# Nine norm statistics in two rounded passes, with the queries' products moved forward and the shared key squares added by GpSimd

## What is computed

```python
def rms_norm(x, gain):
    xf = x.astype(jnp.float32)
    y = xf * lax.rsqrt(jnp.mean(xf * xf, axis=-1, keepdims=True) + RMS_EPS)
    return (y * gain.astype(jnp.float32)).astype(x.dtype)

q_d = rms_norm(heads(d_q, DSA_HEADS), dsa_q_norm)
k_d = rms_norm(heads(d_k, DSA_HEADS), dsa_k_norm)
q_m = heads(rms_norm(m_cq, mla_q_latent_norm) @ mla_w_uq, MLA_HEADS)
k_rope = jnp.broadcast_to(m_kr[:, :, None, :], (B, S, MLA_HEADS, MLA_ROPE_DIM))
q_m = rms_norm(q_m, mla_q_norm)
k_m = rms_norm(jnp.concatenate([k_nope, k_rope], axis=-1), mla_k_norm)
```

## Time and profile before

| | |
|---|---|
| median of three runs | 1244.68 us (1244.66 to 1244.74) |
| the profiled execution: its own time | 1245.98 us |
| the profiled execution: span, first to last instruction | 1244.2 us |
| PE busy in the span | 1232.3 us (99%) |
| DVE, ACT, POOL busy | 757.9 us (61%), 534.4 us (43%), 232.9 us (19%) |
| granted clock of PE | 0.998 of full speed |
| chain that ended last | PE 92%, DVE 3%, ACT 3%, issue 1%, DMA 1% |

### The profile page before, as it was taken

The page is one execution under the profiler, slowest core; times in us unless marked ns, Lnnn a source line. Parts: engine busy times, 40 slices in busy tenths (PEclk is TensorE's granted clock), DMA queues, the critical chain, the costliest instruction groups (busy, mean ns, idle before and its releaser), DMA issues.

```text
span 1244.2 us, 17723 instructions
## 1 busy us (share of the span) xinstructions
PE 1232.3 (99%) x5952; PEld 973.4 (78%) x5952; DVE 757.9 (61%) x1229; ACT 534.4 (43%) x869; POOL 232.9 (19%) x156
## 2 busy tenths in 40 slices
PE   8999999999999999999999999999999999999998
PEld 7767876788888888888886678757888888888887
DVE  6788978644544554544758899685445445445444
ACT  5675448644223224224437653595442242232331
POOL 1035430020120110210520544201202102002002
PEclk9999999999999999999999999999999999999999
DMA  6312220024223223223222222101223223222323
GB/s 232 102 51 68 73 81 2 23 97 132 87 99 100 96 91 101 101 84 101 101 87 84 68 68 85 52 2 51 85 101 102 85 102 101 89 97 100 100 96 108
DMA packets 30721, 108.37 MB, mean 87 GB/s; under 512 B 3536, under 2 KB 3536, under 8 KB 30672
## 3 DMA queue, kind: packets, MB, share of 16 engines
q1 hardware_dynamic: 29520, 103.82, 24.9%
q0 software_dynamic: 432, 2.86, 0.6%
q10 hardware_dynamic: 720, 1.07, 0.3%
HBM read 105.64 MB, written 2.10 MB: 87 GB/s over the span
## 4 chain that ended last, share of the span: by engine, by line
PE 92%; DVE 3%; ACT 3%; issue 1%; DMA 1%; ACTq 0%; DVEq 0%
PE bank L957 19%; PE bank L955 19%; PE bank L956 19%; PE bank L564 6%; PE bank L565 6%; PE bank L566 6%; PE bank L587 2%; PE bank L585 2%; PE bank L586 2%; PE bank L837 1%; PE bank L849 1%; PE bank L600 1%; PE bank L864 1%; PE bank L711 1%; PE bank L815 1%
## 5 line engine op out<-in xcount | busy, mean ns | idle before, releaser
L1010 ACT ACTIVATE wh<-raw 128x1024 fp32r<-128x1024 f32 x191 | 201.7, 1056 | 371.4 <-PE bank L957 246.5
L1341 DVE TENSOR_TENSOR wl<-raw,wh 128x1024 fp32r<-128x1024 f32 x161 | 248.0, 1540 | 76.9 <-ACT wh L1010 76.9
L955 PE MATMUL bank<-hh,wl 128*128 128x512 f32 x512 | 200.0, 391 | 0.0
L955 PE MATMUL bank<-xmh,wl 128*128 128x512 f32 x512 | 199.3, 389 | 0.0
L957 PE MATMUL bank<-hl,wh 128*128 128x512 f32 x512 | 199.2, 389 | 0.0
L957 PE MATMUL bank<-xml,wh 128*128 128x512 f32 x512 | 199.2, 389 | 0.0
L956 PE MATMUL bank<-xmh,wh 128*128 128x512 f32 x512 | 199.2, 389 | 0.0
L956 PE MATMUL bank<-hh,wh 128*128 128x512 f32 x512 | 199.2, 389 | 0.0
L529 POOL TENSOR_TENSOR x<-x,rsb 128x512 f32<-128x512 f32 x62 | 82.0, 1322 | 587.3 <-DVE rsb L1772 587.3
L1761 DVE TENSOR_TENSOR sqb<-tf 128x512 f32<-128x512 f32 x64 | 44.3, 692 | 180.9 <-ACT hh L1305 180.9
L564 PE MATMUL bank<-xgh,wl 128*128 128x512 f32 x368 | 151.6, 412 | 2.8 <-DVE xgl L1354 2.8
(11 more groups left out here) (231 smaller groups left out, 1677.2 us busy)
## 6 DMA issues: line engine op xcount, KB each, us to landing
raw<-in_stream SPq DMA_DIRECT2D x191, 512.0 KB, 3.3
out_y<-x SPq DMA_DIRECT2D x8, 256.0 KB, 3.8
x<-in_x ACTq DMA_DIRECT2D x4, 256.0 KB, 7.1
x<-in_x SPq DMA_DIRECT2D x4, 256.0 KB, 7.1
con<-in_consts POOLq DMA_DIRECT2D x1, 976.5 KB, 5.1
par<-in_params POOLq DMA_DIRECT2D x1, 916.0 KB, 5.2
par<-in_params POOLq DMA_DIRECT2D x1, 896.0 KB, 6.7
raw<-in_stream SPq DMA_DIRECT2D x2, 256.0 KB, 3.9
```

The source lines that it names most:

```text
L955: pe.matmul(B.t[s][:], wl[:, s, n_block(k)], src_h[:, k], start=(k == 0), stop=False)
L1010: act.activation(wh[:, s], raw[:, s], ACT.Copy).then_inc(hi_ready.sem, 1)
L1341: vec.tensor_tensor(wl[:, s], raw[:, s], wh[:, s], ALU.subtract).then_inc(lo_ready.sem, 1)
```

## The change

1. `FIRST_PART` goes from 7 to 3 and `N_PARTS` from 5 to 9: the statistics `mqst0`, `dqst1`, `mqst1` and `dkst0` take the rounded form too. ACT gets one rounding and DVE one `square_low` for each, and PE two float32r matmuls in place of one float32 matmul.
2. The key squares: `turn_rows`, its three memsets and the float32 matmul of line 666 go. ACT squares the shared rotary rows twice into a new buffer `krq` (rows 0 to 31 and 64 to 95, POOL zeroes the rest), POOL adds `krq` to the squares `sqb` of `mk0` and `mk1` (behind its low part of u = 13 and 14), and only then does ACT round them.
3. DVE's order: a new function `queries_of(u)` runs between `evacuations(u)` and `select_steps`. It holds `mla_queries`, `mla_turn` and the `square_low` of u = 9 to 12. `dsa_queries`, `dsa_keys` and all of u = 13 and 14 but `mla_queries(3)` stay in `tasks(u)`, behind the selection.

The diff without the lines that only follow from these:

```diff
-FIRST_PART, N_PARTS = 7, 5
-ACT_LINKS = 2 + N_PARTS
+FIRST_PART, N_PARTS = 3, 9
+ACT_LINKS = 2 + N_PARTS - 2
...
+        krq, _ = place("krq", [P, T], at=gvt0)
-        turn_rows, _ = place("turn_rows", [P, P])
...
# POOL
-                pool.memset(cqn[QK:P, 1], 0.0).then_inc(padded.sem, 1)
+                pool.memset(cqn[64:P, 1], 0.0).then_inc(padded.sem, 1)
                 pool.wait_ge(*padded.at(l, 1))
                 alone(pool)
+                pool.memset(krq[:], 0.0).then_inc(padded.sem, 1)
+                pool.wait_ge(*padded.at(l, 2))
+                alone(pool)
...
+                    if u in (13, 14):
+                        i = norm_index(f"mkst{u - 13}")
+                        pool.wait_ge(*krsq_ready.at(l, 1))
+                        pool.wait_ge(*ksq_ready.at(l, u - 13))
+                        pool.tensor_tensor(sqb[:, i % 2], sqb[:, i % 2], krq[:], ALU.add).then_inc(ksq_summed.sem, 1)
                     if u in (14, 15):
                         key_end(u - 14)
...
# PE
                 def mla_k_stat(pr):
-                    pe.wait_ge(*krsq_ready.at(l, 0))
                     pe.wait_ge(*B.vacant(l, name))
-                    pe.matmul(B[name][:], turn_rows[:], cqn[:, 1], start=True, stop=False)
                     pe.wait_ge(*nsl_ready.at(l, i - FIRST_PART))
-                    pe.matmul(B[name][:], blk_r[:], sqh[:, i % 2], start=False, stop=False)
+                    pe.matmul(B[name][:], blk_r[:], sqh[:, i % 2], start=True, stop=False)
...
-                stat(l, "dqst1", blk, sq_of("dqst1"))
+                stat_parts(l, "dqst1", blk_r[:]).then_inc(*B.on_fill("dqst1"))
-                stat(l, "dkst0", blk, sq_of("dkst0"))
+                stat_parts(l, "dkst0", blk_r[:]).then_inc(*B.on_fill("dkst0"))
...
# ACT
+                def key_square(pr):
+                    i = norm_index(f"mkst{pr}")
+                    act.wait_ge(*B.filled(l, f"mk{pr}"))
+                    act.activation(sqb[:, i % 2], B[f"mk{pr}"][:], ACT.Square).then_inc(ksq_ready.sem, 1)
+                    act.wait_ge(*ksq_summed.at(l, pr))
+                    act.activation(sqh[:, i % 2], sqb[:, i % 2], ACT.Copy).then_inc(nsq_ready.sem, 1)
...
                         act.wait_ge(*kr_ready.at(l, 0))
-                        act.activation(cqn[64:QK, 1], kT[64:QK, 0], ACT.Square).then_inc(krsq_ready.sem, 1)
+                        act.wait_ge(*padded.at(l, 2))
+                        act.activation(krq[0:ROPE], kT[64:QK, 0], ACT.Square).then_inc(krsq_ready.sem, 1)
+                        act.activation(krq[64:QK], kT[64:QK, 0], ACT.Square).then_inc(krsq_ready.sem, 1)
...
# DVE
-            vec.memset(turn_rows[0:64], 0.0).then_inc(rows_ready.sem, 1)
-            vec.memset(turn_rows[64:QK], 1.0).then_inc(rows_ready.sem, 1)
-            vec.memset(turn_rows[QK:P], 0.0).then_inc(rows_ready.sem, 1)
...
+                def queries_of(u):
+                    if 10 <= u <= 13:
+                        mla_queries(u - 10)
+                    if 9 <= u <= 12:
+                        mla_turn(u - 9)
+                        square_low(f"mqst{u - 9}", slice(0, QK))
+                    if u == 9:
+                        square_low("dqst1")
+                    if u in (10, 11):
+                        square_low(f"dkst{u - 10}")
...
                     evacuations(u)
                     if 6 <= u < POOL_LOW[0]:
                         low_part(u % 2, hi_ready.at(l, u + AHEAD))
+                    queries_of(u)
                     select_steps(done, per_slot.get(u, 0))
                     done += per_slot.get(u, 0)
                     tasks(u)
```

More of the change, by code:

```diff
@@ L237, in build_trunk @@
         ke, ke0 = place("ke", [P, 2, TB, 256])
-        gvt, _ = place("gvt", [P, TB, GLA_H * GLA_DV])
+        gvt, gvt0 = place("gvt", [P, TB, GLA_H * GLA_DV])
+        krq, _ = place("krq", [P, T], at=gvt0)
         e1, _ = place("e1", [P, 2, T])
@@ L346, in build_trunk @@
         rows_ready = S("rows_ready", 0)
-        padded = S("padded", 2)
+        padded = S("padded", 3)
+        ksq_ready = S("ksq_ready", 2)
+        ksq_summed = S("ksq_summed", 2)
         cq_summed = S("cq_summed")
@@ L360, in build_trunk @@
         nrs_used = S("nrs_used", N_NORM, start=2)
-        krsq_ready = S("krsq_ready")
+        krsq_ready = S("krsq_ready", 2)
         krg_ready = S("krg_ready")
@@ L646, in mla_q_stat @@
                 def mla_q_stat(h):
-                    if norm_index(f"mqst{h}") < FIRST_PART:
-                        stat(l, f"mqst{h}", ones[0:QK, 0:QK], sq_of(f"mqst{h}")[0:QK], QK)
-                        return
                     pe.wait_ge(*blk_ready.at(0, 0))
@@ L736, in _ @@
                 pe.wait_ge(*B.vacant(l, "cqst"))
-                pe.wait_ge(*rows_ready.at(0, 3))
+                pe.wait_ge(*rows_ready.at(0, 0))
                 pe.matmul(B["cqst"][:], ones[:], sqb[:, 0], start=True, stop=True).then_inc(*B.on_fill("cqst"))
@@ L1074, in square_high @@
                     act.activation(sqh[rows, i % 2], sqb[rows, i % 2], ACT.Copy).then_inc(nsq_ready.sem, 1)
+                def key_square(pr):
[4 more added lines that the diff above has]
+                    act.activation(sqh[:, i % 2], sqb[:, i % 2], ACT.Copy).then_inc(nsq_ready.sem, 1)
                 def query_square(h):
-                    sq = square if norm_index(f"mqst{h}") < FIRST_PART else square_high
-                    sq(f"mqst{h}", B[f"mq{h}"][0:QK, :], slice(0, QK), wait=B.filled(l, f"mq{h}"))
+                    square_high(f"mqst{h}", B[f"mq{h}"][0:QK, :], slice(0, QK), wait=B.filled(l, f"mq{h}"))
                     if h == 0:
@@ L1170, in tasks @@
                         factor("dqst0", DH)
-                        square("dqst1", dqr[:, 1], wait=B.freed(l, "dq1"))
+                        square_high("dqst1", dqr[:, 1], wait=B.freed(l, "dq1"))
                     if u == 10:
@@ L1175, in tasks @@
                         factor("dqst1", DH)
-                        square("dkst0", dkn[:, 0], wait=B.freed(l, "dk0"))
+                        square_high("dkst0", dkn[:, 0], wait=B.freed(l, "dk0"))
                     if u == 11:
@@ L1187, in tasks @@
                         factor("mqst3", QK, QK)
-                        square_high("mkst0", B["mk0"][:], wait=B.filled(l, "mk0"))
+                        key_square(0)
                     if u == 14:
-                        square_high("mkst1", B["mk1"][:], wait=B.filled(l, "mk1"))
+                        key_square(1)
                     if u in (14, 15):
@@ L1566, in tasks @@
                     if u == 9:
-                        mla_turn(0)
                         dsa_queries(0)
                     if u == 10:
-                        mla_queries(0)
-                        mla_turn(1)
                         dsa_queries(1)
                     if u == 11:
-                        mla_queries(1)
-                        mla_turn(2)
-                        square_low("mqst2", slice(0, QK))
                         dsa_keys(0)
-                        square_low("dkst1")
                     if u == 12:
-                        mla_queries(2)
-                        mla_turn(3)
-                        square_low("mqst3", slice(0, QK))
                         dsa_keys(1)
                     if u == 13:
-                        mla_queries(3)
                         vec.wait_ge(*B.filled(l, "krot"))
```

1 line of the change is left out of this document (removed).

## The result

The changed kernel takes 1262.43 us in the median (1261.94 to 1263.55), against 1244.68 before: a ratio of 1.0144 with a 95% interval of 1.0128 to 1.016. It is slower, as forecast, but by 17.8 us where 7.6 were forecast, and outside the range of 1240 to 1257.5. The profiled execution took 1261.94 us with a span of 1260.1, so the two profiled spans differ by 15.9 us.

A forecast was written before the change was run, and what follows sets the result against it. PE was taken as the bound. A layer loses 2.2 us by `mkst1`, 1.4 at the banks and 0.2 at unit 5: 3.8, or 7.6 in all, giving 1253.6 profiled and 1252.3 for the runs; range 1240 to 1257.5.

The forecast's parts named there:

- PE's saving if it never waits: Four statistics from 0.86 to 0.46 us and two keys' statistics without their float32 matmul: 3.3 us a layer, 6.7 in all.
- The kind of loss: PE idle for DVE's `sql`, 2 us and more a layer, `mla_v` waiting for DVE, DVE instructions held beside POOL.
- The rival of the full gain: PE served in time, POOL's work falling beside the selection: 4.8 to 6.2 us faster, 1238.5 to 1240 us; chance 0.2.
- The 0.2 us at unit 5: ACT's second square of the shared rows delays unit 5's block: PE waits 0.2 us a layer, bounds 0.1 and 0.4.
- `mkst1` gives back: At the second key's statistic the low part is in time and PE wins 0.87 us, leaving 2.2 lost a layer.
- `mla_k(1)` starts 0.6 later [...] 3.0 us lost: At `mkst0` the low part ends at 120.3, PE comes at 117.8, `mla_k(1)` starts at 120.9 instead of 117.85.
- the early branch at `mkst0`: DVE's low part of `mkst0` runs ahead of POOL's next one and ends at 120.3: 3.0 us lost a layer.
- the branch that it priced at 5 us a layer: POOL's next low part, from 119.2, gets ahead of `mkst0`'s low part, which then ends at 122.4: 5 us.
- One layer is worked out and doubled: Layer 1 repeats layer 0 614.4 us later, so 3.8 us lost a layer becomes 7.6 in all.
- I estimate 1.4 us for both: `mv0` and `mv1` wait for the keys' banks, as DVE and ACT's factor come later: 1.4 us a layer, bounds 0 and 3.
- The walk of the two queues: DVE's and POOL's queues followed instruction by instruction with the rows' durations, giving ready times where PE waits; 3.8 us lost a layer.
- the later branches: `dsa_queries(1)` behind POOL's low part, `mkst0`'s low behind the next: 5 to 6 us a layer, 1255 to 1257.5 us; chance 0.18.

The follow-up runs named there:

- e7: Changed kernel plus 7, 7 and 12 idle matmuls in PE's waits at `mqst3`, `mkst0` and `mla_v(1)`: 1264.47 us.
- e14: Changed kernel, DVE making POOL's low parts of units 9 to 12, `mkst0`'s low part and ACT's factor earlier, selection thinned there: 1247.75 us.
- e12: Changed kernel, POOL's low parts of units 9 to 15 halved, `mkst0`'s low part before unit 13's selection, ACT's factor before the wait for POOL's addition: 1245.84 us.
- e2: Kernel before plus the key squares' part alone, with five norms in parts and the old DVE order: 1253.01 us.
- e13: Complete changed kernel, `mkst0`'s low part before unit 13's selection and ACT's factor before the wait for POOL's second addition: 1256.09 us.
- e5: Kernel before plus the key squares alone, ACT making `mkst0`'s factor before waiting for POOL's second addition: 1246.11 us.
- e11: Changed kernel with one edit, ACT making `mkst0`'s factor before waiting for POOL's second addition: 1259.53 us median, profiled execution 1253.46.
- e3: Kernel before plus nine rounded statistics alone, old DVE order, new `square_low` behind the selection, `turn_rows` kept: 1256.37 us.
- e9: Changed kernel without key squares, `mkst0`'s rotation and low part before unit 13's selection, selection steps moved from units 9, 11, 12, 13 to 21, 22: 1254.33 us.
- e10: Complete changed kernel, ACT's factor first, `mkst0`'s low part before unit 13's selection, selection steps moved from units 9, 11, 12, 13 to 21, 22: 1264.01 us.
- e16: Changed kernel, DVE making low parts of units 9 to 12, selection thinned, `mkst0` low part, ACT factor and `mla_keys(1)` earlier, one POOL scaling later: 1244.17 us.

## Why the prediction was wrong in size

**What held.** PE's saving if it never waits, 3.3 us a layer: the nearest run to it (1241.04 us) keeps 2.24 at `mla_v(1)`, with small waits at each step. The kind of loss: PE waits at L672 and L682 for DVE, and DVE's held instructions end 0.55 us after POOL's, in all 21 cases of the two layers' blocks in which one took over 1 us. The rival of the full gain named the right condition, that POOL's work and DVE's miss each other; it took half of POOL's low parts away and three orders to meet it. The 0.2 us at unit 5 held too: in all thirteen kernels with the key squares' part the lateness grows by 0.26 to 0.28 us at that unit of layer 1, and in none of the others.

**By terms**, against the forecast of 3.8 us lost a layer (us; the lateness of the table, in its order):

| term of the sum | forecast | layer 0 | layer 1 |
|---|---|---|---|
| up to `mla_k(1)`: the wait for `mkst0` | 3.05 | 4.32 | 6.04 |
| `mkst1` gives back | -0.87 | -0.87 | -0.87 |
| waits for the banks of `mla_v(0)`, `mla_v(1)` | 1.4 | 3.7 | 0.6 |
| half clock behind them or behind `mkst0` | none | 1.7 | 1.7 |
| unit 5 and small rest | 0.2 | 0.4 | 0.0 |
| sum | 3.8 | 9.23 | 7.47 |

The row for the banks is what is left of the growth of lateness from `mla_k(1)` to `mla_v(1)` when the gain of `mkst1` and, in layer 1, the half clock are taken off. So of the 9.1 us that the two layers together were off, 4.3 were missed at `mkst0`, 3.4 in the clock and 1.5 at the banks.

**The first step that failed: "`mla_k(1)` starts 0.6 later [...] 3.0 us lost".** It took the early branch at `mkst0`, in which DVE's low part is not held, for both layers. Its own times speak for the other: a low part that ends at 120.3 starts at 119.6, and POOL's next low part was to start at 119.2, which is ahead of it. That is the branch that it priced at 5 us a layer, and layer 1 took it: POOL started 0.67 us ahead, DVE took 2.71 us, PE waited 4.7 us, and 6.04 were lost. DVE's line and POOL's in the changed kernel, layer 1:

```profile
743.36 2.71 DVE L1440 TENSOR_TENSOR sql<-sqb,sqh 128x512 fp32r<-128x512 f32 x1
```

```profile
742.69 2.84 POOL L505 TENSOR_TENSOR wl<-raw,wh 128x1024 fp32r<-128x1024 f32 x1 [4.58 <-ACT wh L1014]
```

That layer 0 took the early branch was luck: the stretch of half clock at 112.0, which the prediction did not have, held POOL's low part back to 120.65, behind the 120.00 of DVE's. Layer 1 had the same wait of 1.5 us at `mqst3` and no stretch behind it. "One layer is worked out and doubled" could not see this.

**The second: the clock was no term.** Three stretches of 1.2 GHz at 1.7 us each are 5.1 us of PE's time, and two of them reached the end. The one at 112.0 did not: PE still waited 1.36 us at `mkst0` behind it, and DVE waited only 0.17 us from 102 to 120. The one at 139.3 did: lateness is 7.15 at `mla_v(1)` and 8.83 where the logits of the attention begin. So did the one at 746.8: lateness grows by 0.76 from `mla_k(1)` to `mla_v(0)` in layer 1, where it should fall by the 0.87 of `mkst1`. In e7 no stretch stood behind the two waits that were filled whole, which speaks for the wait as what the clock answers to; but waits of 1.5 at `mqst2` (e14), and of 1.9 (e12), 2.7 (e2) and 3.0 (e13) at `mla_v(1)`, brought none, so when a wait brings one is open.

**The third: "I estimate 1.4 us for both".** The waits at the banks took 3.7 us in layer 0 and 0.6 in layer 1. The prediction named ACT's factor behind POOL's addition and gave it nothing of its own. By the runs it is 2.9 us a layer alone (`mla_v(1)` +3.07 in e2, +0.13 in e5), and in layer 0 of the changed kernel 3.2 (+7.15, and +3.9 in e11). Both times about 1.0 us is the factor itself; the rest is that `mla_keys(0)`, so much later, is held by POOL's low part (2.88 us for the line of 129.21; 0.68 in e11). The walk of the two queues stopped short of that meeting. Nor did it look at what DVE does ahead of `mla_keys(1)`: four steps of the selection, some 4 us, with the factor long there. They stood there before the change too, but then PE came only at 131.85.

**The walk was a microsecond optimistic from unit 11 on.** It gave 91.8 for the second low part of that unit; it came at 92.08 in a layer that had started 0.79 earlier, so 1.1 late against the walk: POOL's second scaling (89.81 to 91.54) held it. `mla_q(3)` was forecast 0.45 early and was 0.30 late. That the low part of `mkst0` ended at 120.69, beside the 120.3 written down, owes 0.8 to the earlier start. One count was off without effect: in the stretch from 83 to 116 us POOL has three cosine turns before the change, not four.

**The range** ended with the later branches at 1257.5. It had no case in which the clock came on top of them.

## What to carry to other kernels

An operation that is moved ahead on an engine moves everything behind it, and where two engines share a port the price is paid where the moved work meets the other engine, not where the edit is: walk both queues to the last wait of the block, including each instruction that stands in front of one that frees a bank. Where the walk has two engines start within a microsecond of each other, write both starts down and take the branch that they give, and price the other. A rounding that waits for a third engine should stand behind the results that others already wait for; here one such place on ACT cost 7 us, more than the matmuls it was to save. Before a saving on PE is counted, ask how long PE will stand still for it, since a wait can cost more than its length in clock. And a faster PE starts the other engines earlier: here that brought POOL in ahead of DVE.

## What the runs showed of the hardware

- **Granted clock.** Behind some waits of PE of 1.5 us and more the granted clock was 0.5 (1.2 GHz) for 3.41 us, each such stretch worth 1.7 us. After a single wait it began between 0.2 us before the wait's end (e7) and 2.3 us behind it; where two waits followed each other within 4 us it began inside the second or 0.05 us behind it, and in e3, e9 and e10 it lasted 6.83 us in one layer. The kernels without waits over 1 us in the block (1241.04, 1245.06 and 1246.11 us) had none there, and several with such waits had none either.
- **The shared port by hundredths.** A start 0.04 us behind POOL made DVE's 0.69 us into 2.84. The Trainium skill ("SBUF — State Buffer", Who interferes with whom) has the one that starts first keep the port, and these rows agree, while in the earlier trace rows a DVE instruction that followed on the one before without a gap was served ahead of a POOL instruction already begun. Kernels with DVE near POOL at such a place spread in time: 1253.46 to 1259.94 and 1251.84 to 1258.9 us, where the kernel before on the same chips spreads by 2.1 and 0.8. That the branches at the port are the cause of the spread is argued, not shown, since one run of each kernel has a trace.
- **POOL is held by DVE too.** Its scaling of 1.62 us took 2.85 where DVE's low parts of 0.87 and 1.21 us ran beside it in e16 (POOL from 106.48, DVE from 106.19 and 106.99).
